# Block 0 of the last 32 U tiles computed with x stationary, blocks 1 to 3 of them between the V tiles

## The reference, cut to what matters

```python
u = expert_u[i_blk]
vv = expert_v[i_blk]
act = jax.nn.gelu(jnp.einsum('td,tkd->tk', h_blk, u), approximate=False)
return jnp.einsum('tk,tkd->td', act * g_blk, vv)
```

## Time and profile before

| | |
|---|---|
| median of three executions | 2075.17 us (2071.8 to 2093.76) |
| the profiled execution | 2075.27 us |
| its span, first to last instruction | 2073.5 us |
| mean granted clock of TensorE | 0.954 of full speed |
| busy: PE, weight loads, DVE, ACT, POOL | 2012.5, 1601.0, 1096.2, 682.6, 939.9 us |
| HBM traffic | 368.4 MB, 178 GB/s over the span |

### The profile page before, as it was taken

How to read it: one execution, slowest core, us unless ns; L and a number is a source line. 1 busy time by engine, 2 the same in 40 slices (tenths; PEclk the granted TensorE clock), 3 DMA queues, 4 the chain that set the end, 5 groups by cost and what they waited for, 6 DMA issues and landing times.

```text
span 2073.5 us, 24488 instructions
## 1 busy us (share of the span) xinstructions
PE 2012.5 (97%) x9433; PEld 1601.0 (77%) x9433; DVE 1096.2 (53%) x2127; ACT 682.6 (33%) x1031; POOL 939.9 (45%) x502
## 2 busy tenths in 40 slices
PE   8999999999989999999999999999997999999998
PEld 5787554788777888888888888888885878787786
DVE  4001223401250199895488888600156878897787
ACT  4632222422213323333333333322332333333332
POOL 6442000344416334445333333344488888888530
PEclk9998558999989999999999999999999999999999
DMA  5221000132324234444456666654477999999983
GB/s 187 92 93 60 1 0 11 61 100 89 130 88 132 82 102 149 141 149 141 145 184 195 193 199 193 194 207 148 141 274 260 353 351 335 371 378 333 401 320 122
DMA packets 164774, 368.38 MB, mean 178 GB/s; under 512 B 15266, under 2 KB 80930, under 8 KB 164531
## 3 DMA queue, kind: packets, MB, share of 16 engines
q1 hardware_dynamic: 51264, 184.57, 25.6%
q10 hardware_dynamic: 90866, 115.06, 16.4%
q0 software_dynamic: 22528, 67.19, 8.8%
HBM read 305.96 MB, written 60.82 MB: 177 GB/s over the span
## 4 chain that ended last, share of the span: by engine, by line
PE 74%; POOL 14%; issue 4%; DVE 4%; DMA 4%; ACT 1%; SPq 0%; ACTq 0%; DVEq 0%
PE bank L403 20%; PE bank L405 20%; PE bank L404 20%; POOL weight L365 8%; POOL gat L373 6%; PE bank L645 3%; DMA act<-activation_scratch 3%; PE bank L496 2%; PE bank L518 2%; PE bank L508 1%; PE bank L533 1%; DVE acc L1110 1%; PE bank L499 1%; PE bank L541 1%; DMA gat<-in_expert_v,eidx 1%
## 5 line engine op out<-in xcount | busy, mean ns | idle before, releaser
L353 POOL TENSOR_TENSOR w_lo<-stage,w_hi 128x1024 fp32r<-128x1024 f32 x224 | 543.5, 2434 | 951.2 <-ACT w_hi L703 951.1
L403 PE MATMUL bank<-x_hi,w_lo 128*128 128x512 f32 x1376 | 543.5, 395 | 6.9 <-DVE x_lo L977 4.4
L405 PE MATMUL bank<-x_hi,w_hi 128*128 128x512 f32 x1376 | 537.7, 391 | 0.0
L404 PE MATMUL bank<-x_lo,w_hi 128*128 128x512 f32 x1376 | 537.2, 390 | 0.0
L703 ACT ACTIVATE w_hi<-stage 128x1024 fp32r<-128x1024 f32 x348 | 358.7, 1041 | 23.4 <-PE bank L405 14.2
L403 PE MATMUL bank<-w_hi,wt_lo 128*128 128x512 f32 x768 | 304.0, 396 | 31.1 <-issue 18.5
L403 PEld LDWEIGHTS bank<-x_hi,w_lo 128*128 128x128 f32 x1376 | 259.4, 189 | 61.1 <-DVE x_lo L977 5.3
L404 PE MATMUL bank<-w_lo,wt_hi 128*128 128x512 f32 x768 | 302.3, 394 | 0.0
L405 PE MATMUL bank<-w_hi,wt_hi 128*128 128x512 f32 x768 | 302.2, 393 | 0.0
L405 PEld LDWEIGHTS bank<-x_hi,w_hi 128*128 128x128 f32 x1376 | 259.3, 188 | 55.4
L404 PEld LDWEIGHTS bank<-x_lo,w_hi 128*128 128x128 f32 x1376 | 259.7, 189 | 52.6 <-issue 0.2
(11 more groups left out here) (214 smaller groups left out, 1983.4 us busy)
## 6 DMA issues: line engine op xcount, KB each, us to landing
stage<-in_expert_uT SPq DMA_DIRECT2D x128, 512.0 KB
stage<-in_expert_v SPq DMA_DIRECT2D x128, 512.0 KB
stage<-in_mix_stream SPq DMA_DIRECT2D x84, 512.0 KB
gates<-gate_scratch ACTq DMA_DIRECT2D x32, 768.0 KB
act<-activation_scratch ACTq DMA_DIRECT2D x32, 768.0 KB
activation_scratch<-act_out_a ACTq DMA_DIRECT2D x64, 256.0 KB, 2.3
activation_scratch<-act_out_b ACTq DMA_DIRECT2D x64, 256.0 KB, 2.3
gate_scratch<-gstage_a ACTq DMA_DIRECT2D x6, 2048.0 KB, 11.4
```

The source lines that it names most:

```text
L353: nc.gpsimd.tensor_tensor(w_lo[:, slot, 0:width], stage[:, slot % STAGE, 0:width], w_hi[:, slot, 0:width], ALU.subtract).then_inc(split_do ...
L403: mm(dst, l_lo, r_hi, start=first, stop=False)
L404: mm(dst, l_hi, r_lo, start=False, stop=False)
L405: return mm(dst, l_hi, r_hi, start=False, stop=last)
```

## The change

Let "late" be the last 32 tiles of U (96 to 127) and "early" the first 96.

- Early tiles are scored as before. After each 12 of them comes a unit of four late tiles (`score_unit`): the x part of block 0 is stationary and the four tiles of U stream, 512 columns at a time: 24 matmuls of 512 columns into one bank, tokens x experts. ACT applies gelu and writes it to `activation_scratch`, in a layout of its own (`act_late`), for the gathers of block 0.
- Blocks 1 to 3 of each late tile are scored in the V phase: `score_tile(place, P)`, 24 matmuls of 384 columns, one before the V phase and one more before V tiles 0, 4, 8, and so on up to 120. Their gelu goes to the `act_out` buffers and is used from there; it isn't stored. The V tiles are taken in another order: every fourth one (w % 4 == 3) uses a late tile's activations.
- So each late tile of U is loaded, rounded and split twice: 32 more tiles in the weight stream (`stream` lists it: 288 instead of 256).
- `on_vector`: DVE splits the V tiles with w % 4 != 0. POOL splits those with w % 4 == 0 and all U tiles.
- Activations loaded from HBM in the V phase: 24 units instead of 32. Gates: the same bytes, in 24 units and 8 loads of `late_gates`. The first loads stand behind the last unit of the U phase.
- Row buffers: 5 instead of 8, so a row's gather waits for the pick five before it. Rows are gathered for the picks due one V tile later, not three.
- Gate groups: 96 groups over 46 early tiles, (t - 46) * 96 // 46; so 42 tiles have two and four have three (t = 58, 69, 81, 92). The other due times move earlier by the units that now stand between the tiles.

```diff
-GATHER = 8
-EXP_AT = {9: 0, 20: 1, 32: 2, 44: 3}
-TURN_AT = {27: 1, 39: 2, 50: 3}
-FIRST_GATE = 50
-GATE_SPAN = 48
+GATHER = 5
+EARLY = 96
+LATE = NKEY - EARLY
+RUN = EARLY * UNIT // LATE
+N_UOUT = EARLY + LATE // UNIT
+EXP_AT = {8: 0, 19: 1, 30: 2, 41: 3}
+TURN_AT = {25: 1, 36: 2, 47: 3}
+FIRST_GATE = 47
+GATE_SPAN = 46
...
-FIRST_PICK = 10
-LAST_PICK = 118
-LN_FIRST = 121
+FIRST_PICK = 8
+LAST_PICK = 120
+LN_FIRST = 123
...
-def on_vector(tile):
-
-    return tile >= NKEY + 4
+def early_place(t):
+
+    return t + t // RUN * UNIT
+
+
+def late_unit_place(q):
+
+    return q * (RUN + UNIT) + RUN
+
+
+def late_place(m):
+
+    return NKEY + max(0, 5 * m - 4)
+
+
+def value_place(w):
+
+    return NKEY + 2 + w + min(w // 4, LATE - 2)
+
+
+def is_late(w):
+
+    return w % 4 == 3
+
...
+def on_vector(place):
+
+    return place >= NKEY and any(place == value_place(w) for w in range(NKEY) if w % 4 != 0)
...
-                while acts_due < min(NPICK, 4 * (v - FIRST_PICK + 7), picks_by(v + 3) + 2 * CHUNK_PICKS):
+                while acts_due < min(NPICK, 4 * (w - FIRST_PICK + 7), picks_by(w + 1) + 2 * CHUNK_PICKS):
                     gather_act(acts_due)
                     acts_due += 1
-                while rows_due < picks_by(v + 3):
+                while rows_due < picks_by(w + 1):
                     gather_row(rows_due)
                     rows_due += 1
...
+            def score_unit(place):
+
+                n = first_expert + place
+                s = n % RING
+                for k in range(UNIT):
+                    wait_split(pe, n + k)
+                dst = next_out()
+                for c in range(KC):
+                    w = slice(c * P, (c + 1) * P)
+                    ins = mm3(dst[:], x_hi[:, c, 0:P], x_lo[:, c, 0:P], w_hi[:, s:s + UNIT, w], w_lo[:, s:s + UNIT, w],
+                              c == 0, c == KC - 1)
+                ins.then_inc(quarter_used, UNIT)
...
+            for t in range(EARLY):
+                if t in TURN_AT:
+                    turn_picks(TURN_AT[t])
+                score_tile(early_place(t), 0)
+                for g in range(groups_by(t - 1), groups_by(t)):
                     gate_group(g)
+                if t % RUN == RUN - 1:
+                    score_unit(late_unit_place(t // RUN))
...
+            score_tile(late_place(0), P)
             pe.wait_ge(gm_evac, NGROUP)
             pe.wait_ge(parts_ready, TB - 1)
             for v in range(NKEY - TAIL_TILES):
-                wait_split(pe, first_value + v)
+                if v % 4 == 0:
+                    score_tile(late_place(v // 4 + 1), P)
+                wait_split(pe, first_expert + value_place(v))
...
+            for half in range(2):
+                sc.wait_ge(gm_written[half], 16 * NGB // 2)
+            load_unit(0)
+            load_late_gates(0)
+            load_unit(1)
...
             weigh(0)
+            if on_vector(value_place(1)):
+                split_value(value_place(1))
             for w in range(NKEY):
                 if w + 1 < NKEY:
                     weigh(w + 1)
                 weight_low(w)
-                if w + 3 < NKEY and on_vector(NKEY + w + 3):
-                    split_value(NKEY + w + 3)
+                if w + 2 < NKEY and on_vector(value_place(w + 2)):
+                    split_value(value_place(w + 2))
```

More of the change, by code:

```diff
@@ L202, in build @@
         token = tiny[:, 226:227]
+        late_base = tiny[:, 227:228]
         gsum = tiny[:, 232:240]
@@ L253, in build @@
         first_expert = first_query + HP
-        first_value = first_expert + NKEY
+        tiles = stream()
+        vector_places = [p for p in range(len(tiles)) if on_vector(p)]
         PT_UNITS = ["fq", "fk", "z", "fv", "gk", "sfx", "gq", "tot", "gv0", "gv1"]
@@ L265, in wait_product, with raw_weight @@
                 eng.wait_ge(quarter_used, 4 * STREAMED.index(name) + (r + 1 if by_column else 4))
+        def raw_weight(w):
+            if is_late(w):
+                return act_out[(N_UOUT + w // 4) % 2][:, 0:ND]
+            e = value_tile(w)
+            return act[:, e // UNIT % 2, e % UNIT, :]
         def wait_split(eng, n):
-            tile = n - first_expert
-            if on_vector(tile):
-                eng.wait_ge(value_split, sum(on_vector(k) for k in range(tile + 1)))
+            before = sum(p <= n - first_expert for p in vector_places)
+            if n - first_expert in vector_places:
+                eng.wait_ge(value_split, before)
             else:
-                eng.wait_ge(split_done, n + 1 - sum(on_vector(k) for k in range(tile + 1)))
+                eng.wait_ge(split_done, n + 1 - before)
         block = ctx.enter_context(nc.Block())
@@ L300, in _ @@
                     m += 1
[L301 to L304, removed]
+            for p, (kind, tile) in enumerate(tiles):
+                load(first_expert + p, expert_uT[tile] if kind == "u" else expert_v[tile])
             for t in range(TB):
@@ L946, in normalize @@
                 act_f(sd[:, t:t + 1], mv[:, t, 1:2], ACT.Sqrt, bias=eps_col).then_inc(ln2_sqrt, 1)
-            for v in range(1, NKEY):
+            units = 2
+            for v in range(NKEY):
                 round_weight(v)
-                if v + 3 < NKEY:
-                    ahead(first_value + v + 3)
-                if v % UNIT == 0 and v // UNIT + 1 < NUNIT:
+                ahead(min(first_expert + value_place(v) + 3, first_expert + len(tiles) - 1))
+                if v % 4 == 1:
+                    gelu_out(late_place(v // 4), ND)
+                if units < EARLY // UNIT and v == value_of_early(UNIT * (units - 1) - 1) + 1:
                     sc.wait_ge(wt_done, v)
-                    load_unit(v // UNIT + 1)
+                    load_unit(units)
+                    units += 1
+                if v % 16 == 15 and v + 1 < NKEY:
+                    load_late_gates(v // 16 + 1)
                 if v == LN_FIRST - 2:
@@ L1245, in split_value @@
                                 ALU.subtract).then_inc(value_split, 1)
-            for tile in range(NKEY, NKEY + 3):
-                if on_vector(tile):
-                    split_value(tile)
             weigh(0)
+            if on_vector(value_place(1)):
+                split_value(value_place(1))
             for w in range(NKEY):
```

176 lines of the change are left out of this document (112 added, 64 removed).

## The result

| | before | changed kernel |
|---|---|---|
| median | 2076.57 us (4 runs, 2071.8 to 2093.76) | 2118.49 us (4 runs, 2117.43 to 2120.66) |
| ratio to before, 95% interval | | 1.0171 (1.0124 to 1.0219) |
| profiled execution | 2075.27 us | 2117.43 us |

The change made the kernel 1.7% slower (the medians of these few runs lie 2.0% apart, which is inside the interval). The forecast was 2080 us, in a range of 2048 to 2112, with "within 1%" as the likeliest outcome. The measured time lies above the range.

The account below looks back on a forecast made before the run. PE, busy for 97% of the span, was taken as the bound, with POOL's gathers pacing the V phase. 2075.3 + 2.6 (PE's work) + 14.1 (gate groups) - 11.9 (V losses 32.6, not 44.5) = 2080 us; range 2048 to 2112.

Parts of the forecast that it names:

- PE's work, +2.6 us: Matmuls on PE: U phase loses 130.6 us, V phase gains 133.2 us at 173.4 ns per 384-column matmul.
- Rival C: Matmuls of 384 columns cost as much as 512, so 2080 + 41 = 2121 us; chance 0.04.
- Gate groups, +14.1 us: U phase: PE waits 3.52 us for DVE's one-hots at each of four tiles with three groups; bounds 5 and 20 us.
- The clock behind waits: PE's lower clock after idling: 2 us added at the V phase's transition and 2 us in the burst.
- Transition, 11.6 us: Start of V phase: PE idles 9.6 us for first loads behind the last unit's gelu, plus 2 us of lower clock.
- Burst, middle and end, 21 us: V phase losses: 10 us from POOL's early gathers, 8 us over 20 groups of four V tiles, 3 us at the end.
- A: Faster rival: V middle, burst and end lose nothing, gate groups cost only 5 us; 2050 us, chance 0.20.
- B: Slower rival: V phase, PE waits for POOL's splits behind gathers that keep 1.84 us; 2104 us, chance 0.26.

Follow-up runs that it names:

- e3_early_load: Changed kernel with the V phase's first loads of gates and activations issued ahead of the last unit's gelu; ratio to before 1.0217, beside 1.0171 for the changed kernel.
- e14_skip_all_v_early: Changed kernel without gate groups behind units, DVE splitting all V tiles but one, plus first V loads issued before the last unit's gelu; ratio 0.9899, against 0.9843 without early loads.

## Why the prediction was wrong

- **PE's work, +2.6 us: right.** Matmuls of 384 columns start 0.173 us apart in the changed kernel (1419.02, 1419.54 for every third one). Rival C fell. The test in the prediction, that a weight load "would have to exceed 173 ns to bind", doesn't hold by the length of its record: the records of these loads last 190 ns in the trace (0.19 us for the one at 1804.35 us, between two matmuls of 384 columns), and still the matmuls start 173 ns apart.
- **Gate groups, +14.1 us: this step failed.** The trace says 48.7. The third groups made PE wait as the working gave, 3.5 us four times, and cost 20 us with the clock by the U phases of two runs (18 by their ratios). What was mis-sized stands in the prediction as its high bound, "after each of four units POOL splits four tiles in a row, and DVE comes 1 to 2 us late: 20 us". It is 4.6 us of idle time each, and some 7 us each with the clock behind it (the U phase without groups behind a unit is 46.1 us shorter, of which 20 are the third groups). That TENSOR_TENSORs of the two engines exclude each other was in the same text and was used for one split beside one group. Carried through it comes near the size: of a row of splits directly behind each other DVE gets one operation done for each split, so the five operations of a group last about as long as POOL's row of four, 9.8 us instead of 4, and PE is 0.90 + 9.8 - 1.36 - 5.44 = 3.9 us late. In the trace they took 10.6 us (1019.47 to 1030.05).
- **The clock behind waits** was priced in the V phase (2 us each) and left out in the gate stretch, where eight waits of 3.5 and 4.6 us stood; it came to 1.4 to 3.1 us behind each.
- **Transition, 11.6 us: right in kind, high in size.** PE idled 6.0 us, not 9.6. The gates were asked for 2.9 us after the unit and not 5.2, since ACT issues a DMA without waiting for the roundings before it to end (at 1417.70 us, with the last of the four roundings still to start at 1418.38), and the activations were there 8.7 us later, not 10.1.
- **Burst, middle and end, 21 us:** PE's idle time was 15.9 us to 1540 us (5.9 of them the transition), 6.3 us in the middle and 1.1 at the end. All V losses together, 36.9 us, are within 5 us of the forecast's 32.6, but partly by luck, as the path was another. The burst was to make PE wait for POOL's `w_lo` around V tiles 8 to 16; in the trace PE waits for that once, 1.1 us, and ten times, 22.1 us with the transition, for DVE's `wt_lo`. What makes DVE late was left out: the picks, which I let run beside POOL's splits, are shut out by them too (1646 ns for one, not 1284; 46 us over 128 picks). Against that, gathers were cheaper than before (1.48 us in the middle, 1540 to 1900 us, against 1.56).
- **The rivals.** A's premise, that the stretched V phase loses nothing but its start, came true only with the V splits on DVE. B had PE waiting for splits behind gathers and over 50 us lost: the V phase lost 36.9 us, less than the 44.5 before, and a gather in the middle (1.48 us) lies between the sign for A (below 1.3) and the sign for B (1.55 and more). The part of B that came true is that a pick doesn't run beside a split. The slower outcome came from a stretch for which there was no slower rival at all. I had looked for rivals in the V phase, because the losses of before were there; the change adds its bursts where nothing was lost.

## What to carry to other kernels

When a change makes a stream arrive in bursts (here four tiles freed at once), ask who shares a port or an engine with the burst's work, and add the whole burst to what stands beside it; here DVE had 1.3 us of rest in a 7 us cycle and couldn't take it. Try first to place the other engine's work where the burst isn't, before pacing the burst itself: here the first took 26 us off the U phase beside the 20 us of the third groups, and pacing 14. A step whose bounds are 5 and 20 us and whose premise was never priced with its own rule is where the range should be widest.

## What the runs showed of the hardware

DVE's `add_pick` is a SCALAR_TENSOR_TENSOR with two operands in SBUF. It runs beside gathers (1.28 us), but not beside a TENSOR_TENSOR of POOL: in the changed kernel the picks that meet a split, about a quarter of them, take 2.8 us on average, and all others 1.28. One of them, in order of time:

```profile
1806.20 4.75 POOL L421 TENSOR_TENSOR w_lo<-stage,w_hi 128x1024 fp32r<-128x1024 f32 x2
1808.28 3.77 DVE L1229 SCALAR_TENSOR_TENSOR acc<-gat,weight,acc 128x1024 f32<-128x1024 f32 x1 [4.17 <-DMA gat<-in_expert_v,eidx]
```

It started at 1808.28 and ended at 1812.05, 1.1 us after the second split (1810.95). The Trainium skill (SBUF — State Buffer, on the shared port pair) names just this case, a DVE operation with two SBUF inputs against a GpSimd operation that reads SBUF, and says that the loser blocks. The trace agrees, with these numbers; the prediction had left `add_pick` to rival B and out of its own sum.

An idle time of 3.5 us on PE was followed by a granted clock of 1.2 GHz: behind the wait that ended at 1390.68 us the 12 gate matmuls still took 0.86 us, at 2.4 GHz (24 take 1.56), and the matmuls of 512 columns behind them started 0.43 us apart until 1394.7 us. Behind a 4.6 us wait the gate matmuls themselves were slow, 1.46 us for 12.

A store that ACT issues behind 3.8 MB of its own loads lands late: 256 KB took 7.4 us in e3_early_load and about 15 in e14_skip_all_v_early, where such stores take 2.3 us at the median. Weight tiles were loaded at the same time, so how much of the delay is due to ACT's loads isn't shown.
